# A two-layer hybrid decoder step: the barrier between projection and attention stream taken out, the convolution's taps handed out anew

## The reference

```
xn = rmsnorm(x); z = xn @ w_in                      # 1024 -> 2448 columns, split into groups
A  fox:  q,k rms-normed; logf = log_sigmoid(f + b); causal attention, 4 heads of 64,
         scores + cumsum(logf)[q] - cumsum(logf)[k]
B  conv: glu = ga * sigmoid(gb); depthwise convolution of width 31; layernorm; silu
C  nsa:  gates g; q (4 heads) and 6 key/value rows, rms-normed and rotated; attention over
         compressed blocks of 32, over the 16 best blocks of 64, and over a window of 512
D  gmlp: u * (tril(ws) @ layernorm(v) + bs), in chunks of 128
h = x + concat(rmsnorm(A), rmsnorm(B), rmsnorm(C), rmsnorm(D)) @ w_out
y = h + square(relu(rmsnorm(h) @ w_ff1)) @ w_ff2
```

## Time and profile before

| | us |
|---|---|
| median of 3 runs (3616.86 to 3621.1) | 3618.96 |
| the profiled execution | 3620.73 |
| its span, first to last instruction | 3618.6 |
| PE busy in the span | 3300.4 (91%) |
| DVE busy | 1485.9 (41%) |
| ACT busy | 1011.7 (28%) |
| POOL busy | 208.2 (6%) |
| mean granted TensorE clock | 0.964 |

### The profile page before, as it was taken

How to read it: one execution, slowest core, us unless ns; L and a number is a source line. 1 busy time by engine, 2 the same in 40 slices (tenths; PEclk the granted TensorE clock), 3 DMA queues, 4 the chain that set the end, 5 groups by cost and what they waited for, 6 DMA issues and landing times.

```text
span 3618.6 us, 55613 instructions
## 1 busy us (share of the span) xinstructions
PE 3300.4 (91%) x22450; PEld 1880.7 (52%) x22450; DVE 1485.9 (41%) x2775; ACT 1011.7 (28%) x1794; POOL 208.2 (6%) x136
## 2 busy tenths in 40 slices
PE   5989958888889999999998996888897999999998
PEld 3455536666544444444444553566665444444444
DVE  4965553333454321232168564433335443113321
ACT  2123214444533210221101231344444332012211
POOL 0211110000100000000002111000002000000000
PEclk8999969999999999999999997999998999999999
DMA  6423251432221121123143324242332212111222
GB/s 200 138 82 96 78 159 64 141 132 77 76 92 47 52 59 35 42 60 91 48 137 95 98 89 131 70 141 108 95 114 68 71 47 70 47 29 46 76 77 80
DMA packets 379859, 313.02 MB, mean 87 GB/s; under 512 B 125597, under 2 KB 362810, under 8 KB 372538
## 3 DMA queue, kind: packets, MB, share of 16 engines
q1 hardware_dynamic: 372234, 209.13, 20.6%
q0 software_dynamic: 7424, 101.19, 7.6%
HBM read 264.87 MB, written 50.46 MB: 87 GB/s over the span
## 4 chain that ended last, share of the span: by engine, by line
PE 79%; DVE 10%; ACT 4%; issue 2%; SPq 2%; DMA 2%; POOL 1%; POOLq 0%; DVEq 0%; ACTq 0%
PE PS L951 43%; PE PS L1065 9%; PE PS L1323 5%; PE PS L1342 5%; DVE arena L1893 4%; PE PS L1219 3%; PE PS L980 2%; PE PS L1356 1%; PE PS L1040 1%; PE PS L1387 1%; PE PS L1265 1%; DVE arena L2176 1%; ACT arena L1628 1%; PE PS L1226 1%; PE PS L1231 1%
## 5 line engine op out<-in xcount | busy, mean ns | idle before, releaser
L951 PE MATMUL PS<-arena 128*128 128x512 bf16 (+1 forms) x10080 | 1549.1, 317 | 0.0
L951 PEld LDWEIGHTS PS<-arena 128*128 128x128 bf16 x10080 | 753.4, 98 | 794.7
L1065 PE MATMUL PS<-arena 128*128 128x512 f32 (+3 forms) x1152 | 479.2, 572 | 0.0
L1498 ACT ACTIVATE arena<-arena 128x1024 bf16<-128x1024 f32 (+1 forms) x112 | 145.4, 1300 | 1096.8 <-PE PS L951 1076.7
L1065 PEld LDWEIGHTS PS<-arena 128*128 128x128 f32 (+1 forms) x1152 | 209.2, 185 | 237.5 <-issue 204.7
L2455 DVE TENSOR_TENSOR arena<-PS,arena 128x1088 f32<-128x1088 f32 (+1 forms) x48 | 62.0, 1292 | 654.8 <-PE PS L951 631.0
L2181 DVE TENSOR_REDUCE arena<-PS 128x1 f32<-128x1024 f32 (+5 forms) x192 | 138.7, 723 | 358.0 <-PE PS L1326 357.8
L1323 PE MATMUL PS<-arena 128*128 128x512 f32 (+3 forms) x576 | 230.7, 508 | 16.9 <-ACT arena L1637 15.7
L2479 DVE SCALAR_TENSOR_TENSOR arena<-PS,arena 128x1088 f32<-128x1088 f32 x64 | 82.7, 1292 | 354.7 <-PE PS L951 354.3
L1342 PE MATMUL PS<-arena 128*128 128x64 f32 x1632 | 214.2, 277 | 0.0
L1342 PEld LDWEIGHTS PS<-arena 128*128 128x128 f32 x1632 | 202.0, 196 | 9.0 <-issue 5.9
(11 more groups left out here) (335 smaller groups left out, 2886.5 us busy)
## 6 DMA issues: line engine op xcount, KB each, us to landing
arena<-in_w_ff SPq DMA_DIRECT2D x64, 512.0 KB, 4.1
arena<-in_w_ff SPq DMA_DIRECT2D x32, 1024.0 KB, 5.9
arena<-in_cache_nsa_kv SPq DMA_DIRECT2D x256, 64.0 KB
x_s<-arena SPq DMA_DIRECT2D x24, 544.0 KB, 3.5
arena<-x_s SPq DMA_DIRECT2D x2, 4352.0 KB, 13.1
arena<-in_w_in SPq DMA_DIRECT2D x4, 2048.0 KB, 14.7
arena<-in_w_out SPq DMA_DIRECT2D x16, 512.0 KB, 4.2
arena<-in_w_in SPq DMA_DIRECT2D x12, 512.0 KB, 5.8
```

The lines of the kernel that those rows point to most:

```text
L951: last = mm(PS[:, 1536 * k + a:1536 * k + a + wd], ww[:, c, :], xx[:, c, a:a + wd], start=c == 0 and n == 0, stop=c == blocks - 1 and n == 2)
L1065: last = mm(PS[0:r, c * 512:c * 512 + b - a], XNT[:, j, t * P:t * P + r], Wt[:, j, a:b], start=j == 0, stop=j == KD - 1)
L1498: run(WH[k][:, 0:blocks, :], src[k][:, 0:blocks, :], ACT.Copy).then_inc(S["w_hi"], 1)
```

## The change

- **Barrier.** The `arrive` of all engines between projection and stream goes. In its place stand single waits: SP waits for the landing of all stores of the eight prompt tiles and for the last projection matmul before it loads `KV4`; PE waits for `kvc_ready` before it transposes `kv`, and for the last copies of `z` before the scores.
- **Order on SP.** Tiles 0 to 7, `y_s`, then `KV4`, `head_in(0)` and `GH`; then tile 8's stores, the two stores of the convolution's last rows, the wait for all of them, and then the sample loads. `sparse_in(0)` no longer waits for `tot_ready`.
- **Order on PE.** `kv` and `q` of head 0, `scores(0)`, `scores(1)`, and only then `small(QT, 0)` and the tail transposes, then unit 0. The product for `LAT` (`lateness`) goes to unit 5.
- **Order on DVE.** `compressed_done` (L2099 to L2102 before) runs inside tile 8's norms, while POOL takes the power. `row_max(0)` and `row_max(1)` follow `finish` of tile 8 directly; then `stream_setup`; `gates_of_new` stands at the head of unit 3, `gate_totals` of unit 4, `later_sums` of unit 5.
- **POOL.** The memsets of `PADDED` run after tile 8's power and `kvc_mm`; `fox_in(0)` follows them and `y_out`; `fox_in(1)` waits for `tot_ready`.
- **ACT.** The copies of the convolution's last rows follow `probs(0)`. All `kv` groups and head 0's `q` groups are copied by ACT.
- **Extras.** `dk` to `rk` move from units 0 to 8 to units 3 to 11. `FIRST` goes from 7 to 9, and with it all requests and merges; SP's step at unit 9 goes to 12.
- **Taps.** `TAPS_FIRST` goes from 18 to 9, `SUMS_OF` from tiles 2 to 6 to tiles 3 to 7.
- **Layout.** What tile 8 still needs and what the stream needs early no longer share words of `arena`; the small products of tile 8 go to PSUM bank 7.

```diff
-        FIRST, EVERY = 7, 10
+        FIRST, EVERY = 9, 10
...
-            here += {0: [("dk",), ("dq",)], 1: [("vc", 0), ("vc", 1)], 2: [("cd",)], 3: [("ce",)], 4: [("cn",)], 5: [("ci",)],
-                     6: [("co",), ("rk", 0), ("rk", 1)], 7: [("rk", 2), ("rk", 3)], 8: [("rk", 4), ("rk", 5)]}.get(u, [])
+            here += {3: [("dk",), ("dq",)], 4: [("vc", 0), ("vc", 1)], 5: [("cd",)], 6: [("ce",)], 7: [("cn",)], 8: [("ci",)],
+                     9: [("co",), ("rk", 0), ("rk", 1)], 10: [("rk", 2), ("rk", 3)], 11: [("rk", 4), ("rk", 5)]}.get(u, [])
...
-        EVAC_BY = ["ACT" if key[0] in ("sc", "dk", "vc", "kt", "pt") else
-                   ("DVE", "ACT")[g % 2] if key[0] in ("kv", "q", "p") else "DVE" for g, key in enumerate(GROUPS)]
+        EVAC_BY = ["ACT" if key[0] in ("sc", "dk", "vc", "kt", "pt", "kv") or key[0:2] == ("q", 0) else
+                   ("DVE", "ACT")[g % 2] if key[0] in ("q", "p") else "DVE" for g, key in enumerate(GROUPS)]
...
-        SUMS_OF = {2: [(1, 0), (1, 1)], 3: [(1, 2), (2, 0)], 4: [(2, 1), (2, 2)], 5: [(3, 0), (3, 1)], 6: [(3, 2)]}
+        SUMS_OF = {3: [(1, 0), (1, 1)], 4: [(1, 2), (2, 0)], 5: [(2, 1), (2, 2)], 6: [(3, 0), (3, 1)], 7: [(3, 2)]}
...
-        TAPS_GLU, TAPS_FIRST, TAPS_TILE = 22, 18, (4, 3, 4)
+        TAPS_GLU, TAPS_FIRST, TAPS_TILE = 22, 9, (4, 3, 4)
...
-                each_tile(store_step)
-                sp.wait_ge(S["tail_ev"], 1)
...
-                arrive(sp, "sp")
+                for t in range(QT):
+                    store_tile(t, t % 2)
+                sp.wait_ge(S["y_fin"], 3)
+                sp.dma_start(y_s, Yc.rearrange("p c n -> p (c n)")).then_inc(S["y_out"], 16)
...
+                for k in range(2):
+                    sp.wait_ge(S[f"st{k}"], 16 * 11 * (QT // 2))
+                sp.wait_ge(S["z_mm"], 4 * (QT + 1))
                 sp.dma_start(KV4.rearrange("p t g d -> p t (g d)"),
...
                 head_in(0)
                 sp.dma_start(GH, g_s[0:SEQ].rearrange("(t p) c -> p t c", p=P)).then_inc(S["gate_in"], 16)
+                store_tile(QT, 0)
+                sp.wait_ge(S["tail_ev"], 1)
...
+                sp.wait_ge(S["st0"], 16 * (11 * (QT // 2 + 1) + 1))
+                sp.wait_ge(S["tail_out"], 32)
                 sp.dma_start(QS[0:NS], qa_s[SEQ:ROWS, :, 0:HD]).then_inc(S["q_in"], 16)
...
-                sp.wait_ge(S["tot_ready"], 1)
                 sparse_in(0)
...
-                    if u == 9:
+                    if u == 12:
                         sp.wait_ge(S["rank_ready"], 1)
...
-                small(8, 0)
...
-                arrive(pe, "pe")
...
+                def lateness():
+                    pe.wait_ge(S["fin"], QT + 1)
+                    pe.wait_ge(S["tot_ready"], 1)
+                    mm(bank(7, NH * NB), C("later"), TOT.rearrange("p h b -> p (h b)"), start=True, stop=True).then_inc(S["lat_mm"], 1)
+
+                pe.wait_ge(S["kvc_ready"], 1)
                 pe.wait_ge(S["kv4_in"], 16)
...
+                pe.wait_ge(S["z_ev"], 8 * (QT + 1))
                 pe.wait_ge(S["pad_ready"], 4)
...
                 scores(0)
                 scores(1)
+                small(QT, 0)
+                tails()
                 for u in range(NU):
+                    if u == 5:
+                        lateness()
...
+                def compressed_done():
+
+                    dve.wait_ge(S["kvc_mm"], PIECES + 1)
...
-                    rstd(SS18[0:r, :], SS18[0:r, :], HD, "row", t + 1, lambda: [conv(half) for half in taps_of(t, 1)])
+                    rstd(SS18[0:r, :], SS18[0:r, :], HD, "row", t + 1, lambda: [conv(half) for half in taps_of(t, 1)] if t < QT else compressed_done())
...
-                V.memset(MX, -3e38)
-                for key in GROUPS[:10]:
-                    group_out(key)
-                later_sums()
-                gates_of_new()
                 row_max(0)
                 row_max(1)
+                stream_setup()
                 for u in range(NU):
                     h, v = u // UH_, u % UH_
+                    if u == 3:
+                        gates_of_new()
+                    elif u == 4:
+                        gate_totals()
+                    elif u == 5:
+                        later_sums()
...
+                pool.wait_ge(S["piece_next"], 1)
                 pool.wait_ge(S["kvc_mm"], PIECES + 1)
-                fox_in(0)
-                everyone()
...
                     G.memset(PADDED[HD:P, n * 2 * SEQ:(n + 1) * 2 * SEQ], 0.0).then_inc(S["pad_ready"], 1)
                 pool.wait_ge(S["pad_ready"], 4)
+                pool.wait_ge(S["y_out"], 16)
+                fox_in(0)
+                pool.wait_ge(S["tot_ready"], 1)
                 fox_in(1)
```

More of the change, by code:

```diff
@@ L267, in build_step @@
         YM = [CPO, GLS.rearrange("p c b n -> p (c b n)")]
-        heads_at = base + 27830
-        lo = Layout(arena, heads_at, ARENA_W)
+        lo = Layout(arena, base, ARENA_W)
+        PADDED = arena[:, base:base + 8 * SEQ]
+        QFT = [lo.take(SEQ) for _ in range(2)]
+        KFT = [lo.take(SEQ) for _ in range(2)]
+        QNT = [lo.take(SEQ) for _ in range(2)]
+        KST = lo.take(SEQ)
+        KWT = lo.take(SEQ)
+        VREP = lo.take(P, i=4, n=NPB)
+        VBD = lo.take(4 * HD, i=4, d=HD)
+        NMX = [lo.take(24) for _ in range(2)]
+        RS = [lo.take(24) for _ in range(2)]
+        assert lo.at <= after_xnt
+        lo.at = after_xnt
         QF = lo.take(QT * AUG, t=QT, d=AUG)
@@ L367, in build_step @@
         lo = Layout(arena, kp_at + NPG * GW, ARENA_W)
+        WFO = [lo.take(KD * P, k=KD, n=P) for _ in range(2)]
         YB = lo.take(2 * ROWS, c=2, n=ROWS)
-        WFO = [lo.take(KD * P, k=KD, n=P) for _ in range(2)]
         SQG = lo.take(2 * QT * HD, g=2, t=QT, d=HD)
@@ L581, in pair_of @@
             return n // 2 - 1
+        SMALL_BANK = (5, 7)
         def each_tile(step):
@@ L1696, in _ @@
                 probs(0)
+                act.wait_ge(S["tail_T"], 1)
+                run(CPO[0:CW - 1, 0:GW], bank(6, GW)[0:CW - 1], ACT.Copy)
+                run(CPO[0:NS, GW:2 * GW], bank(6)[0:NS, GW:2 * GW], ACT.Copy).then_inc(S["tail_ev"], 1)
                 for u in range(NU):
@@ L2116, in _, with stream_setup @@
-                dve.wait_ge(lfp_in, 128 * l + 128)
-                for h in range(NH):
-                    last = V.tensor_tensor_scan(PFX[:, h].rearrange("p b r -> p (b r)"), C("within"), LF2[:, :, h], 0.0, ALU.mult, ALU.add)
-                last.then_inc(S["dve_done"], 1)
-                dve.wait_ge(S["dve_done"], chain.next())
-                V.tensor_copy(TOT, PFX[:, :, :, NPG - 1]).then_inc(S["tot_ready"], 1)
+                chain.restart()
+                def stream_setup():
+                    dve.wait_ge(S["kvc_ready"], 1)
+                    V.tensor_copy(VREP[HD:P],
+                                  KVC[HD:P, 512:544].unsqueeze(1).to_broadcast([HD, 4, NPB])).then_inc(S["vb_ready"], 1)
+                    for x in GU:
+                        V.memset(x, 1.0)
+                    V.memset(VBD, 0.0).then_inc(S["dve_done"], 1)
+                    dve.wait_ge(S["dve_done"], chain.next())
@@ new lines, in gate_totals @@
+                def gate_totals():
+                    V.memset(MX, -3e38)
+                    dve.wait_ge(lfp_in, 128 * l + 128)
+                    for h in range(NH):
+                        last = V.tensor_tensor_scan(PFX[:, h].rearrange("p b r -> p (b r)"), C("within"), LF2[:, :, h], 0.0, ALU.mult, ALU.add)
+                    last.then_inc(S["dve_done"], 1)
+                    dve.wait_ge(S["dve_done"], chain.next())
+                    V.tensor_copy(TOT, PFX[:, :, :, NPG - 1]).then_inc(S["tot_ready"], 1)
```

130 lines of the change are left out of this document (44 added, 86 removed).

## The result

| | us |
|---|---|
| kernel before, median | 3620.0 |
| kernel after, median (3581.7 to 3593.3) | 3586.4 |
| ratio, 95% interval | 0.9908 (0.9888 to 0.9928) |
| profiled executions, before and after | 3620.7, 3587.9 |

The forecast was 3552, from 3532 to 3577. The gain is real, 0.9%, but 34 us stand where 68 were summed, and the time lies outside the range. The rest of this part asks where the other 34 us went.

A forecast was written before the change was run, and what follows sets the result against it. TensorE was taken as the bound, with time to win only where it stands still or runs at its low clock. Gains of 10.5 and 26 less 2.7 gave 33.8 us a layer, 67.6 in both: 3552 us, range 3532 to 3577.

The forecast's parts named there:

- the taps: Projection, tiles 0 to 2: fewer half taps ahead of tile 0 gain 10.5 us a layer, bounds 5 to 14.
- the border: Projection to stream: without the barrier the stream starts earlier, gain 26 us a layer, bounds 18 to 29.
- the end: Second barrier: the last merge moves into the last unit, loss 2.7 us a layer, bounds 0 to 6.
- faster: Whole kernel: the first four cases, all with a shorter time than before, were given 0.94 together.
- each by 3.1 us: Projection: tiles 1 and 2 bound by VectorE, 36.3 us a tile against TensorE's 33.1.
- the rival itself names: Unit 3: the last sample load lands after 12 us, 9 us less gain a layer, 3570; chance 0.14.
- The COPY that was to wait for the fourth memset: Tile 8's norms: a VectorE COPY waits for the end of POOL's fourth memset, 1.6 us.
- the rival by which they wait for memsets: Tile 8's norms: TENSOR_TENSORs wait for memsets too, about 1 us a layer, 3554; no chance of its own.
- `sparse_in(0)` and `head_in(1)` come earlier than now: Loads for the stream: both issued earlier than in the kernel before, with no cost counted.
- I take 0: Stream between: requests meet other units, a shift of up to 4 us either way possible, counted as 0.
- pairs of groups copied by one engine: Stream: six more neighbouring groups (148 for 142) evacuated by one engine, at 0.7 each a loss up to 4 us.
- the wait at unit 3 hardly shows and the clock stays up: Rival, unit 3 and `q` transposes: less waiting, high clock, 15 us more gain in both layers, 3537; chance 0.14.

The follow-up runs named there:

- experiment 3: Kernel after with 13 half taps ahead of tile 0 and 9 in each of tiles 0, 1 and 2, for 9 and then 11, 11, 9: 3574.6 us.
- experiment 6: Kernel of experiment 1 with all that needs the sample loads (`dk` to `rk`, `gates_of_new` and the steps behind) two units later: 3557.1 us.
- experiment 1: Kernel after with the second head's loads, `head_in(1)`, ahead of `sparse_in(0)` on SP: 3570.5 us.
- experiment 4: Kernel before with `FIRST` 9 for 7 and nothing else, so all requests and merges two units later: 3660.9 us.
- experiment 5: Kernel of experiment 1 with `FIRST` back to 7: 3560.7 us.
- experiment 7: Kernel of experiment 1 with `EVAC_BY` chosen by a search so that fewer neighbouring groups are copied by one engine: 3582.6 us.
- experiment 9: Kernel of experiment 8 with `mo 0` and `mo 1` in one unit and `mo 2` one unit earlier, out of the last unit: 3551.4 us.
- experiment 2: Kernel before with nothing but the new taps (`TAPS_FIRST` 9 for 18, `SUMS_OF` one tile later): 3607.8 us.
- experiment 12: Kernel of experiment 8 with each request's three `pt` groups one unit behind its `ex`, and `pv` one unit behind them: 3543.3 us.
- experiment 8: Kernel after with the edits of experiment 1, experiment 3 and experiment 6 together: 3553.3 us.

## Why the prediction was half right

**Where the 34 us are.** Set against the forecast stretch by stretch, both layers together, the taps (A) fell short by 4 us, the border and the stream (B to E) by 28, and the end (F) by 1. So the mechanisms of the barrier, the taps and the end were right, and the miss is in what the prediction put at nothing behind unit 7. It had given the outcome "faster" 0.94, and that came; the time it named missed by as much as was gained.

**The taps: 10.5 forecast, 7.7 and 9.2 measured, 9.0 alone.** The wait of tile 1 went, and two waits of 2.8 and 3.0 us came at tiles 2 and 3, in size and place as forecast. The step that failed is "each by 3.1 us": from one `finish` to the next it was 37.7 us, not 36.3. The missing 1.4 us a tile are the 32 matmuls behind each wait, 3.53 and 3.38 us for 1.96 in layer 1: `finish` waits for `small`, which stands behind them on TensorE. In layer 2 the waits are the same, 2.75 and 2.96 us, but only the second is followed by a slow product (1.96 and 3.47 us), and the gain is 9.2 us instead of 7.7. I had read exactly this in the earlier trace rows (3.68 for 1.96) and counted it as gone with the old wait. In experiment 3 no slow product is left, and the projection is 7.0 and 5.5 us shorter.

**The border: 26 forecast, right up to unit 7.** From the last projection matmul to `scores(7)` it was 54.3 us; the forecast was 55.6, the kernel before took 81.5. The key load was issued 1.1 us after the projection and not 3, since the stores had landed; `q` came 13.9 us after it, `scores(2)` 25.2 for 28.0; VectorE stood at `gates_of_new` for the sample loads, and TensorE with it for 6.9 us, where I had about 5. That wait was priced; experiment 6 shows that it could have been avoided. (The lower bound of this term should have been 17 and not 18: a last load that takes 12 us for 3 costs the 9 us that the rival itself names.)

The COPY that was to wait for the fourth memset did so: it took 1.19 us for 0.28 and ended when the memsets did, at 453.8. DVE beside four memsets (446.73 to 453.76) in tile 8's norms:

```profile
446.81 0.67 DVE L1972 TENSOR_TENSOR arena<-arena 64x512 f32<-64x512 f32 x1
...
449.04 0.82 DVE L1982 TENSOR_TENSOR arena<-arena 64x640 f32<-64x640 f32 x1
...
452.65 1.19 DVE L1997 COPY arena<-arena 64x192 f32<-64x192 f32 x1
```

None of the TENSOR_TENSORs was stretched to a memset's 1.8 us. By the Trainium skill, "SBUF — State Buffer", section "Who interferes with whom", an operation with two SBUF inputs passes beside a GpSimd instruction that only writes; the trace agrees, and the rival by which they wait for memsets is out.

**Behind unit 7: "`sparse_in(0)` and `head_in(1)` come earlier than now", taken as nothing.** This is the step that failed most. They do come earlier, 15.8 us for `head_in(1)` (507.7 for 523.5), but its user in unit 9 comes 37 us earlier (508.6 for 545.7) and stands 6.2 us, 7.7 in layer 2. I had followed SP to the sample loads and no further, and compared each load with its own old time instead of with its user's new one. Cost: 16 us in both layers (experiment 1).

**The stream between: 0 forecast with up to 4 either way, 5.9 and 5.6 measured in D.** "I take 0" failed too. Idle time gives 2.6 and 3.2 us of it. The shift by two units is the likely cause, as it gave 2.6 and 2.9 in the kernel before (experiment 4), though undoing it here gave only 1.4 and 1.8 back (experiment 5). The cause that I had named, pairs of groups copied by one engine, is neither shown nor refuted. By the order that the code makes, `FIRST` 9 for 7 gives D six more pairs copied by VectorE (36 for 30) and two more by ScalarE, and in layer 1 the waits for VectorE's copies rise from 16.6 to 19.2 us, those for ScalarE's from 25.5 to 26.1. In experiment 7 thirteen more pairs of VectorE go with 6 us more idle time. Both come to some 0.4 to 0.5 us a VectorE pair, which is an estimate and no test; 34 copies more for VectorE in experiment 7 against 2 here do not stand in that proportion. The other 4.4 and 3.0 us are low clock, a term that my sum did not have. With it the shift alone, sized at 5.4 us for both layers, cost 42 us in the kernel before (experiment 4) and 10 in the changed one (experiment 5).

**The end: 2.7 forecast, 3.6 and 3.0 measured.** Right, as far as shown. VectorE's last instruction ends 2.4 us ahead of SP's 16 request loads, which end at 983.51; it was the other way round before. `FIRST` 7 alone takes F from 25.4 back to 22.9. Whether the last merge is the cause, experiment 9 does not settle: it brought 1.9 us back in layer 1 and 0.2 in layer 2.

**The low clock.** In the six stretches it costs 50 us in the kernel before and 60 in the kernel after, both layers. Idle time fell by 42 us, and one would think that the low clock falls with it. It did at the border (4 us) and in the projection (6), and rose by 18 in C and D. The rival "the wait at unit 3 hardly shows and the clock stays up" had the sign wrong: TensorE's one long hole was replaced by a shorter one and holes of 5 to 8 us in units 3 and 9, and C has 11.1 and 8.5 us of low clock for 5.3 and 3.9. Experiments 1 and 6 took these two away and with them 11 us of low clock out of C (19.6 in after, 15.3 in experiment 1, 8.6 in experiment 6, both layers).

**Still open.** In stretch D the idle time of the kernel after and of experiments 1, 3 and 4, all with `FIRST` 9, is 46.4 to 46.9 us in either layer, while the low clock takes 4.6 to 12.5 us. It comes in spells of some 4 to 8 us, and their places recur: in the kernel after and in experiment 1 they begin about 36, 88, 142, 220, 305, 345, 363 or 378 us into D, but each layer of each trace has only some of them. With `FIRST` 7 (before and experiments 2 and 5) the low clock takes 3.3 to 6.6. That more of it belongs to the shift is likely, as no value lies above 6.6 there, but not shown: experiments 7 and 12 have `FIRST` 9 and 4.8 and 6.3, 1.4 and 4.8 us. Why a spell begins at one of these places in one layer and not in the other, no run here shows. The 26 us of low clock in experiment 4 are measured and not explained.

## What to carry to other kernels

When a barrier goes, compare every load with the new time of its user, down to the end of the queue, not with its own old time: an issuing engine that was early for everybody becomes the bound, and the order of its list is the cheapest thing to change (16 us here for moving two lines). Spread the fine work so that the slower engine needs no more per tile than the faster one: here four waits of 2.8 to 3.0 us in two layers brought three slow products, and one wait of 1.8 us brought none. Book the low clock apart from idle time: it took 0 to 16 us a stretch here, and a range that leaves it out is too narrow.

## What the runs showed that I had not expected

- **The idle time is reproducible, the low clock is not.** Idle time in stretch D repeats to 0.5 us between layers and between kernels with the same steps there; the low clock's share differs nearly threefold between the two layers of one execution (12.5 and 4.6 us in experiment 1, with 46.4 and 46.7 us idle):

```profile
517.30:907.20 389.90, 343.55 (x3377) 253.28 (x3375) 136.87 (x390) 164.79 (x378) 14.05 (x14) 0.96 0.30 98
2263.90:2646.10 382.20, 335.53 (x3378) 247.35 (x3376) 136.89 (x390) 164.46 (x378) 14.06 (x14) 0.99 0.30 100
```

  The five executions of experiment 8 spread over 16 us, 0.46%, and their mean granted clock goes with it: 0.978 at 3543.7 and 3544.3 us, 0.971 to 0.973 at 3553.3 to 3560.2. By the Trainium skill, "TensorE: Matmul & The Clock Gate", part 1, the number of slow matmuls varies from run to run of the same kernel; these clocks agree, and here that is as large as the effect of a whole edit.
- **One and the same list of instructions** stayed at 1.2 GHz to 534 instead of 515 when only steps behind it had changed (experiment 4, layer 1).
- **Filling idle time** raised the clock as wanted (12 transposes in 1.47 us for 2.82) and gained nothing measurable where another engine set the pace.
- **Issues on SP.** 16 page loads with their addresses read from a table take 18.6 us of SP, 1.17 each; the plain loads behind them take 0.4 to 1.2.
